# First high parts of w_out made inside RWKV's last step, finer turns of rows and norm steps, gates times norm weights on GpSimd

## The reference: what is computed

```
y_ssd, y_rwkv, y_ml = three mixers on u = norm(x) @ w_in       # 512 + 256 + 256 features
y_rwkv = group_norm(o_f + o_b + bonus, centred, 4 heads) * rwkv_norm_g * gate
x = x + g1 * (concat(y_ssd, y_rwkv, y_ml) @ w_out)             # 1024 x 1024
x = x + g2 * ffn(norm(x))
```

## Time and profile before

| | |
|---|---|
| median of 3 timed executions | 2269.94 us (2266.12 to 2270.01) |
| profiled execution | 2261.78 us, its span 2260.1 us |
| PE busy | 2102.5 us, 93% of the span |
| DVE, ACT, POOL busy | 859.8, 773.8, 753.9 us (38, 34, 33%) |
| mean granted clock of PE | 0.965 of full speed |
| share of the chain that ended last | PE 83%, DVE 6%, ACT 5% |
| idle of PE that a low part of weights by POOL ended (L1016) | 21.2 us, 8 times |

### The profile page before, as it was taken

The page is one execution under the profiler, slowest core; times in us unless marked ns, Lnnn a source line. Parts: engine busy times, 40 slices in busy tenths (PEclk is TensorE's granted clock), DMA queues, the critical chain, the costliest instruction groups (busy, mean ns, idle before and its releaser), DMA issues.

```text
span 2260.1 us, 45965 instructions
## 1 busy us (share of the span) xinstructions
PE 2102.5 (93%) x20444; PEld 1961.6 (87%) x20452; DVE 859.8 (38%) x1435; ACT 773.8 (34%) x1375; POOL 753.9 (33%) x561
## 2 busy tenths in 40 slices
PE   7999998888889999999979989888888899999999
PEld 6999766777789999999979987577778899999998
DVE  5845267565540111011148452765554311101112
ACT  4535444433242222121154364533332422222212
POOL 5432163223223333332323222632232233333331
PEclk8999989999889999999989999989999899999999
DMA  7553200000112222244326431000002122222222
GB/s 255 183 160 103 60 8 20 3 26 24 38 56 66 75 76 76 76 128 133 94 84 196 131 116 31 1 20 17 12 23 66 47 75 75 75 75 73 73 73 73
DMA packets 255259, 169.32 MB, mean 75 GB/s; under 512 B 23872, under 2 KB 228222, under 8 KB 255062
## 3 DMA queue, kind: packets, MB, share of 16 engines
q1 hardware_dynamic: 254835, 166.32, 24.6%
q10 hardware_dynamic: 227, 0.07, 0.0%
HBM read 162.21 MB, written 4.15 MB: 74 GB/s over the span
## 4 chain that ended last, share of the span: by engine, by line
PE 83%; DVE 6%; ACT 5%; issue 2%; POOL 2%; SPq 1%; DMA 0%; another core or an unknown queue 0%; DVEq 0%; ACTq 0%; POOLq 0%
PE PS L1016 21%; PE PS L1018 21%; PE PS L1017 21%; PE PS L1424 5%; PE PS L974 2%; ACT arena L1926 1%; POOL ring_r L694 1%; SPq L455 1%; PE PS L1446 1%; PE PS L1494 1%; ACT whi_r L1755 1%; DVE U L2465 1%; PE PS L1527 1%; PE PS L1082 1%; ACT arena L1971 1%
## 5 line engine op out<-in xcount | busy, mean ns | idle before, releaser
L1016 PE MATMUL PS<-rwp_r,whi_r 128*128 128x320 f32 x2880 | 910.7, 316 | 46.0 <-POOL ring_r L694 21.2
L1018 PE MATMUL PS<-rwp_r,ring_r 128*128 128x320 f32 x2880 | 901.1, 313 | 0.0
L694 POOL TENSOR_TENSOR ring_r<-ring,whi_r 128x1024 fp32r<-128x1024 f32 (+1 forms) x204 | 498.3, 2444 | 1103.6 <-ACT whi_r L1755 1103.6
L1017 PE MATMUL PS<-arena_r,whi_r 128*128 128x320 f32 x2240 | 699.5, 312 | 0.0
L1016 PEld LDWEIGHTS PS<-rwp_r,whi_r 128*128 128x128 f32 x2880 | 551.6, 192 | 62.9 <-issue 29.5
L1018 PEld LDWEIGHTS PS<-rwp_r,ring_r 128*128 128x128 f32 x2880 | 551.1, 191 | 0.0
L1017 PEld LDWEIGHTS PS<-arena_r,whi_r 128*128 128x128 f32 x2240 | 427.7, 191 | 0.0
L1755 ACT ACTIVATE whi_r<-ring 128x1024 fp32r<-128x1024 f32 (+1 forms) x204 | 211.3, 1038 | 536.6 <-PE PS L1018 536.5
L1017 PE MATMUL PS<-U_r,whi_r 128*128 128x320 f32 x960 | 300.7, 313 | 0.0
L2705 DVE TENSOR_TENSOR U<-arena,PS 128x640 f32<-128x640 f32 x44 | 36.2, 822 | 554.2 <-PE PS L1018 554.2
L1017 PEld LDWEIGHTS PS<-U_r,whi_r 128*128 128x128 f32 x960 | 184.3, 192 | 0.2
(11 more groups left out here) (402 smaller groups left out, 2619.5 us busy)
## 6 DMA issues: line engine op xcount, KB each, us to landing
ring<-in_ffn_w SPq DMA_DIRECT2D x120, 512.0 KB, 3.7
rwp<-in_ada_w SPq DMA_DIRECT2D x64, 512.0 KB, 4.8
ring<-in_w_in SPq DMA_DIRECT2D x50, 512.0 KB, 4.3
U<-in_ada_w SPq DMA_DIRECT2D x16, 512.0 KB, 8.3
ring<-in_w_out SPq DMA_DIRECT2D x16, 512.0 KB, 4.1
arena<-in_ada_w SPq DMA_DIRECT2D x16, 512.0 KB, 4.5
ring<-in_ffn_w SPq DMA_DIRECT2D x16, 384.0 KB, 3.4
out<-arena SPq DMA_DIRECT2D x5, 512.0 KB, 2.6
```

The lines of the kernel that those rows point to most:

```text
L694: g.tensor_tensor(rings_r[:, slot_of[n], 0:size(n), :], slot(n)[:, 0:size(n), :], whis[:, q % 2, 0:size(n), :].bitcast(F32), ALU.subtract) ...
L1016: mm(out, w[0][:, k, :], hi[:, cols], start=start, stop=False)
L1017: mm(out, w[0][:, k, :], lo[:, cols], start=False, stop=False)
L1018: return mm(out, w[1][:, k, :], hi[:, cols], start=False, stop=stop)
```

## The change

ACT makes the high parts of w_out's blocks 0 and 1 in RWKV's last step, behind `y_high(range(3, 4))`, instead of behind the whole step; POOL's `low_part` of both thus moves too, behind `gates()`. POOL then multiplies the gates by the norm weights (`gate_gains`). DVE adds the bonus for each tile alone (g_src is counted twice), multiplies the centred y by the gates and weights while it would wait for the std, and has one product for each tile left after 1/std is spread. PE's rows stand in finer turn: row 0, sums of y, row 1, sums of squares, rows 2 and 3, spread, rows 4 and 5, then rows 6 and 7 of block 0 and then those of block 1. Block 2 begins with the two passes that need only high parts of weights, in a loop of its own, and its third pass follows.

```diff
--- before.py
+++ after.py
@@ -98,9 +98,9 @@
 POOL_CONST = DEPTH + 10
 POOL_IDENT, POOL_SET = DEPTH + 3, 87
 PER_LAYER = {
-    "bc_exp": 30, "bc_mm": 30, "bonus": 1, "cs_mm": 5, "cs_read": 5, "dec_diag": 1, "dec_mm": 1, "dec_read": 1,
+    "bc_exp": 30, "bc_mm": 30, "bonus": 2, "cs_mm": 5, "cs_read": 5, "dec_diag": 1, "dec_mm": 1, "dec_read": 1,
     "ec_mm": 12, "ec_read": 12, "ex_in": 64, "feat_ready": 18, "ffn_mm": 44, "ffn_ready": 22, "ffn_silu": 22,
-    "g_mm": 7, "g_read": 4, "g_rec": 1, "g_sq": 2, "g_src": 1, "g_std": 1, "gated": 5, "inv_add": 50,
+    "g_mm": 7, "g_read": 4, "g_rec": 1, "g_sq": 2, "g_src": 2, "g_std": 1, "gated": 5, "inv_add": 50,
     "inv_copy": 50, "inv_mm": 80, "k_scaled": 2, "kk_sq": 2, "lora_in": 48, "lora_x": 2, "num_half": 4,
     "num_mm": 5, "out_ready": 1, "pair_mm": 38, "pair_read": 38, "pl_ready": 10, "qk_mm": 5, "rf_ready": 2,
     "rf_t": 2, "rhs_act": 10, "rhs_mm": 20, "row_in": 112, "rows_act": 7, "rows_dve": 3, "rows_hi": 1,
@@ -767,6 +767,13 @@
                             ins = g.tensor_scalar(U[:, Z + f, :], U[:, Z + f, :], col(lay, "rwkv_r_k", f), None, ALU.mult)
                         ins.then_inc(s["bonus"], 1)
 
+                    def gate_gains():
+
+                        for f in range(2):
+                            ins = g.tensor_scalar(U[:, LORA + f, :], U[:, LORA + f, :], col(lay, "rwkv_norm_g", f), None,
+                                                  ALU.mult)
+                        ins.then_inc(s["bonus"], 1)
+
                     def end_values(c):
 
                         pool.wait_ge(s["ta_act"], at["ta_act"] + 4 * c + 3)
@@ -894,6 +901,8 @@
                             rwkv()
 
                         low_part(lay * Q_LAYER + q)
+                        if q == Q_WOUT + 1:
+                            gate_gains()
 
             @block.tensor
             def _(pe):
@@ -1582,12 +1591,12 @@
                             ins = mm3(PS[:, b + hf, 0:HALF], w, k, hi, lo, halves[hf], start, stop)
                         return ins
 
-                    def out_rows(seq):
+                    def out_rows(seq, blocks=(0, 1)):
 
                         for n in seq:
                             k = YSEQ[n]
                             pe.wait_ge(s["y_lo"], at["y_lo"] + n + 1)
-                            for m in range(2):
+                            for m in blocks:
                                 ins = residual_mm(4 + 2 * m, w01[m], k, rp_r[:, k, :], U_r[:, YTILES[k], :], n == 0,
                                                   n == KT - 1)
                                 if n == KT - 1:
@@ -1597,19 +1606,19 @@
                     for f in range(2):
                         g_job(2 * f, [(BO[:, :], U[:, Z + f, :])]).then_inc(s["g_mm"], 1)
                     w01 = [split_block(Q_WOUT + m) for m in range(2)]
-                    out_rows(range(3))
-                    pe.wait_ge(s["g_src"], at["g_src"] + 1)
+                    out_rows(range(1))
                     for f in range(2):
+                        pe.wait_ge(s["g_src"], at["g_src"] + f + 1)
                         g_job(2 * f, [(BO[:, :], U[:, BT_ + f, :])]).then_inc(s["g_mm"], 1)
-                    out_rows(range(3, 4))
+                    out_rows(range(1, 2))
                     for f in range(2):
-                        pe.wait_ge(s["g_read"], at["g_read"] + 4)
+                        pe.wait_ge(s["g_read"], at["g_read"] + 3)
                         pe.wait_ge(s["g_sq"], at["g_sq"] + f + 1)
                         for hf in range(2):
                             ins = mm(PS[64 * hf + 32 * f:64 * hf + 32 * f + 32, 0, 0:HALF], BO[:, 48:80],
                                      gtmp[:, f, halves[hf]], start=True, stop=True)
                     ins.then_inc(s["g_mm"], 1)
-                    out_rows(range(4, 6))
+                    out_rows(range(2, 4))
                     pe.wait_ge(s["g_rec"], at["g_rec"] + 1)
                     for f in range(2):
                         for hf in range(2):
@@ -1617,8 +1626,30 @@
                             ins = mm(PS[:, 2 * f + hf, 0:HALF], SPREAD[rows, :], gtmp[rows, 3, 0:HALF], start=True,
                                      stop=True)
                         ins.then_inc(s["g_mm"], 1)
-                    out_rows(range(6, 8))
-                    for m in range(2, KT):
+                    out_rows(range(4, 6))
+
+                    for m in range(2):
+                        out_rows(range(6, 8), (m,))
+
+                    def split_late(q):
+
+                        pe.wait_ge(s["split_hi"], q0 + q + 1)
+                        return whis[:, (q0 + q) % 2, :, :]
+
+                    w_hi = split_late(Q_WOUT + 2)
+                    pe.wait_ge(s["wo_read"], at["wo_read"] + 1)
+                    for k, t_ in enumerate(YTILES):
+                        for hf in range(2):
+                            for n, y_ in enumerate((rp_r[:, k, :], U_r[:, t_, :])):
+                                mm(PS[:, 4 + hf, 0:HALF], w_hi[:, k, :], y_[:, halves[hf]], start=k == 0 and n == 0,
+                                   stop=False)
+                    w = split_block(Q_WOUT + 2)
+                    for k in range(KT):
+                        for hf in range(2):
+                            ins = mm(PS[:, 4 + hf, 0:HALF], w[1][:, k, :], rp_r[:, k, halves[hf]], start=False,
+                                     stop=k == KT - 1)
+                    ins.then_inc(s["wo_mm"], 1)
+                    for m in range(3, KT):
                         w = split_block(Q_WOUT + m)
                         pe.wait_ge(s["wo_read"], at["wo_read"] + m - 1)
                         for k, t_ in enumerate(YTILES):
@@ -1984,6 +2015,9 @@
                             decays(k + 1)
                         else:
                             y_high(range(3, 4))
+
+                            split(q0 + Q_WOUT)
+                            split(q0 + Q_WOUT + 1)
                         for l in range(2):
                             copies(3 + l, 4 + 2 * l)
                             if k == NC - 1:
@@ -2007,8 +2041,6 @@
                                 s["yn_std"], 1)
                         if k == NC - 2:
                             y_high(range(3))
-                    split(q0 + Q_WOUT)
-                    split(q0 + Q_WOUT + 1)
 
 
                     A(NSD[:, :], NRC[:, :], ACT.Sqrt)
@@ -2651,6 +2683,9 @@
                         dve.wait_ge(s["g_mm"], at["g_mm"] + f + 1)
                         v.tensor_tensor(pair(gtmp[:, 6 + f, :]), PS[:, 2 * f:2 * f + 2, 0:HALF],
                                         pair(U[:, RV_ + f, :]), ALU.mult).then_inc(s["g_read"], 1)
+                        dve.wait_ge(s["g_read"], at["g_read"] + f + 1)
+                        v.tensor_tensor(U[:, BT_ + f, :], U[:, BT_ + f, :], gtmp[:, 6 + f, :], ALU.add).then_inc(
+                            s["g_src"], 1)
 
                     def centre(t_, b, n):
 
@@ -2658,22 +2693,22 @@
                         v.scalar_tensor_tensor(out=pair(U[:, t_, :]), in0=PS[:, b:b + 2, 0:HALF], scalar=-1.0 / 64,
                                                in1=pair(U[:, t_, :]), op0=ALU.mult, op1=ALU.add).then_inc(
                             s["g_read"], 1)
-                    dve.wait_ge(s["g_read"], at["g_read"] + 2)
-                    v.tensor_tensor(U[:, BT_:BT_ + 2, :], U[:, BT_:BT_ + 2, :], gtmp[:, 6:8, :], ALU.add).then_inc(
-                        s["g_src"], 1)
-                    dve.wait_ge(s["g_src"], at["g_src"] + 1)
+                    dve.wait_ge(s["g_src"], at["g_src"] + 2)
                     for n in range(2):
                         centre(BT_ + n, 2 * n, 3 + n)
+
+                    dve.wait_ge(s["bonus"], at["bonus"] + 2)
+                    dve.wait_ge(s["g_read"], at["g_read"] + 4)
+                    for f in range(2):
+                        ins = v.tensor_tensor(U[:, LORA + f, :], U[:, BT_ + f, :], U[:, LORA + f, :], ALU.mult)
+                    ins.then_inc(s["dve_step"], 1)
                     dve.wait_ge(s["g_std"], at["g_std"] + 1)
                     v.reciprocal(gtmp[:, 3, 0:HALF], gtmp[:, 3, 0:HALF]).then_inc(s["g_rec"], 1)
-                    for f, gate in enumerate((LORA, MISC)):
-                        y_ = U[:, BT_ + f, :]
+                    dve.wait_ge(s["dve_step"], step())
+                    for f in range(2):
                         dve.wait_ge(s["g_mm"], at["g_mm"] + 6 + f)
-                        v.scalar_tensor_tensor(out=pair(y_), in0=pair(y_), scalar=col(lay, "rwkv_norm_g", f),
-                                               in1=PS[:, 2 * f:2 * f + 2, 0:HALF], op0=ALU.mult,
-                                               op1=ALU.mult).then_inc(s["dve_step"], 1)
-                        dve.wait_ge(s["dve_step"], step())
-                        v.tensor_tensor(y_, y_, U[:, gate, :], ALU.mult).then_inc(s["y_done"], 1)
```

(2 more changed lines are left out.)

## The result

The changed kernel takes 2239.68 us (median of 4, 2231.28 to 2248.04) against 2268.85 us for the kernel before beside it: a ratio of 0.989, 95% interval 0.9858 to 0.9921. It was forecast faster by 22 us and became faster by 29. On a second chip the ratio was 0.9874 (0.9844 to 0.9905). Single executions of one kernel on one chip lie up to 26 us apart (2256.66 to 2283.02 us for the kernel before, at mean granted clocks of 0.969 and 0.954), so the trace, in which the changed stretch repeats to 0.01 us, says more about the mechanism than the medians.

The account below looks back on a forecast made before the run. PE's stalls and low clock between RWKV's last step and w_out's third block bound it: 29.2 us to gain, less 0.2 (ACT), 5.5 (POOL and DVE) and 1.5 (clock), takes 22.0 off 2269.94, giving 2247.9 us; range 2238 to 2257.

Parts of the forecast that it names:

- The sum of the work: From the first head sums to the end of block 2, a PE that never waits needs 27.7 us at full clock.
- (a) to (f): Splits, norm chain and block 2: each link ready before PE needs it, so stalls of 2.32, 4.22 and 2.71 us go.
- The gain in the stage: First head sums to end of block 2: 16.0 + 13.2 = 29.2 us of stalls, low clock and small gaps to be had.
- The splits on ACT: RWKV's last step: ACT's two moved splits make its copy 0.2 to 0.4 us late, costing 0.1 us a layer.
- the turns of POOL and DVE: RWKV's last step: POOL and DVE alternate whole instructions, making PE 2.75 us late in each layer, 5.5 us in all.
- part 2: What the moved work holds up in RWKV's last step: ACT 0.1 us a layer, POOL and DVE 5.5 us, clock 1.5 us.
- rival B: RWKV's last step: DVE keeps its turn and RWKV isn't held; 29 us gained, 2241 us; chance 0.22.
- The clock term: RWKV's end: a new PE idle of 2.75 us may bring a low grant, costing 1.5 us, bounds 0 and 3.5.

## Why the prediction was right, and where it was not

**The sum of the work** was right: 27.7 us forecast, 27.62 and 27.63 measured, with every link (a) to (f) under its cover. The reciprocal started 572.98 - 571.55 = 1.43 us behind the sums of squares, as before; the two products by the gates cost nothing.

**The gain in the stage** was right: 29.2 us forecast, 29.3 in the same two profiles, 27.5 against another profile of before. The difference of 1.8 us is low clock behind the stalls, which varies between executions.

**The splits on ACT** cost nothing. From RWKV's 64x256 matmuls of the last step to the first head sums it is 565.35 - 538.35 = 27.00 us before and 563.54 - 536.54 = 27.00 after; 0.1 us a layer was forecast. The first copy behind the splits did come 0.3 us late, as forecast, and the next one was on time again.

**The step that failed is the turns of POOL and DVE** (part 2): 5.5 us forecast, nothing measured, rival B's result. I took the full turns of two low parts and two TENSOR_TENSOR of weights for a rule of all POOL's work and laid the difference at DVE's semaphore waits. The right reading of the earlier trace rows was the other one: the TENSOR_SCALAR had let DVE's product pass because of its form. Waits stood between the low parts in every experiment, and they lost whole turns to TENSOR_TENSOR only. With what the runs showed, the forecast's own timeline gives DVE's first low part 0.7 us behind POOL's second TENSOR_TENSOR, then three of 0.75 us and one hold of 0.5 us: 554.2 + 3.0 + 0.5 = 557.7 and the first add at 558.1 us, in time for PE at 558.17, which is what came. If the form had been TENSOR_TENSOR, PE would have been held 1.24 and 0.90 us. So even then 2.75 us a layer was too much: I had let each of the two instructions hold DVE for its 1.87 us, and the two-input form held it 1.87 - 0.81 = 1.1 us.

**The clock term**, 1.5 us, hung on that hold and fell with it. Its bound of 3.5 us for both layers was too narrow for the hold as such: the run with four more TENSOR_TENSOR lost 6.5 us in layer 0 and 1.5 in layer 1 to 0.50. Behind 1.24 us of idle time one run lost nothing, behind 1.26 us another lost 1.5 us.

**The profiled time** of 2239.8 us that the forecast named came out at 2239.41, but by luck: 7 us more were gained in the stages and 4 us elsewhere, and 11 us were lost to low clock in layer 1's mixers in that one execution. The medians are the fair comparison: 2247.9 forecast, 2239.7 measured, inside the range because the range took in rival B, whose 2241 us it is near. The direction and the stage were right by their mechanism; of the sum's two terms against the gain, 5.5 and 1.5 us, neither came.

The Trainium skill (SBUF — State Buffer, section Who interferes with whom) has VectorE instructions with two SBUF inputs blocked by any GpSimd instruction that reads SBUF, for all of it. The trace agrees for TENSOR_TENSOR of GpSimd (holds of 1.1 to 2.2 us, until the instruction ended) and not for TENSOR_SCALAR: it reads SBUF too, and DVE's low parts ran beside it in 0.82 us or were held 0.5 us. The prediction said that the trace agreed for both forms; the earlier trace rows already spoke against that, since DVE's product started 0.5 us behind the TENSOR_SCALAR and wasn't held. The measurement decides.

## What to carry to other kernels

Before costing work that moves to GpSimd beside VectorE, look up its form: a two-input instruction took a full turn from a two-input instruction of VectorE, a one-input one held it by 0.5 us at most here, also with four more of them in the queue. Sum a PE-bound stretch from its own matmul spacing and lay each link of the side chain against it; that sum was right to 0.1 us. And weigh a stall by more than its length: the low clock behind it was worth from nothing to 6.5 us, and differed between executions of the same kernel.

## What the runs showed of the hardware that was not expected

A TENSOR_SCALAR of 128x640 on GpSimd took 1.88 us alone, and also when two of DVE's two-input products began 0.6 us or more behind its start (the rows at 1652.00 and 547.87 us). It took 2.9 to 3.1 us when one of DVE's was already running at its start and another followed at once; DVE lost at most 0.5 us. That the two meet only in a first part of the instruction fits these rows, but no run was made for it. A TENSOR_TENSOR of 128x1024 took 2.35 us alone and 2.93 after waiting for one of DVE's, and DVE's 2.97 instead of 0.82 after waiting for it. What inside GpSimd makes the difference wasn't tried.

The granted clock was 0.50 for 16 us in one layer behind an idle time of 2.48 us and for 3 us in the other behind 2.19; it was 0.64 in the mean over the 4.7 us behind one of 2.32 us, 0.51 over the 3.2 us behind one of 1.26, and 1.00 behind one of 1.24. Behind the stall of 2.71 us it was 0.50 in some executions and 1.00 in others. Idle time alone doesn't tell; these runs don't settle what does.
